# A decoder layer on one core: late blocks of attention keep the values as weights, search behind the low parts, every superblock splits its own weights

## The reference, cut to what matters

```
h = rms_norm(x);  proj = h @ w_in            # q, k, v, qi, ki, wi and the four HGRN parts
iscore[t,s] = sum_h wi[t,h] * relu(qi[t,h] . ki[s])          # 8 indexer heads of 64
idx = top_k(causal iscore, 256)                              # per query
o[t,h] = softmax(q[t,h] . k[idx] / 8) @ v[idx]               # 8 heads of 64, 2 KV heads
mix = concat(o, hgrn2(...)) @ w_out;   x = x + rms_norm(mix)
h2 = rms_norm(x);  ff = (silu(h2 @ w_gate) * (h2 @ w_up)) @ w_down       # inner width 2816
out = x + rms_norm(ff)
```

## Time and profile before

| | |
|---|---|
| median of 3 runs | 3363.38 us (3362.57 to 3368.68) |
| profiled execution | 3364.6 us |
| its span | 3362.8 us |
| mean granted TensorE clock | 0.984 |
| PE, PEld busy | 95%, 84% |
| DVE, ACT, POOL busy | 60%, 38%, 7% |
| HBM read and written | 393.41 MB, 132.71 MB |

### The profile page before, as it was taken

How to read it: one execution, slowest core, us unless ns; L and a number is a source line. 1 busy time by engine, 2 the same in 40 slices (tenths; PEclk the granted TensorE clock), 3 DMA queues, 4 the chain that set the end, 5 groups by cost and what they waited for, 6 DMA issues and landing times.

```text
span 3362.8 us, 46208 instructions
## 1 busy us (share of the span) xinstructions
PE 3198.6 (95%) x17928; PEld 2822.9 (84%) x17928; DVE 2020.8 (60%) x3427; ACT 1284.1 (38%) x2117; POOL 237.1 (7%) x400
## 2 busy tenths in 40 slices
PE   8999999999889899999889999998999999989998
PEld 7999999998777788878778888887888888868886
DVE  4467778788566776666676555567855653341223
ACT  3454445455466454444443333335433332210000
POOL 0001000000111110000110001011100000010000
PEclk9999999999899899999999999999999999989999
DMA  5543343443323556565643343345333333465554
GB/s 183 163 129 133 132 142 113 132 133 123 115 86 127 187 203 225 212 227 217 244 152 128 134 142 140 129 162 200 125 125 125 123 116 126 154 242 195 175 211 165
DMA packets 167658, 529.15 MB, mean 157 GB/s; under 512 B 17296, under 2 KB 38160, under 8 KB 165392
## 3 DMA queue, kind: packets, MB, share of 16 engines
q1 hardware_dynamic: 165136, 522.00, 44.9%
q10 hardware_dynamic: 2304, 4.20, 0.3%
HBM read 393.41 MB, written 132.71 MB: 156 GB/s over the span
## 4 chain that ended last, share of the span: by engine, by line
PE 58%; DVE 6%; DMA 5%; ACT 2%; issue 2%; SPq 0%; DVEq 0%; POOL 0%; ACTq 0%; POOLq 0%
PE PJ_d L2130 8%; PE PJ_d L2132 8%; PE PJ_d L2131 8%; PE SC L2083 6%; PE PJ_d L2155 6%; PE PJ_d L2157 6%; PE PJ_d L2156 6%; PE SA L2042 3%; PE SA L2069 3%; PE SA L2043 3%; DMA split_d<-wd 3%; DVE score L1773 1%; DVE prob L1867 1%; DVE h_lo L1887 1%; ACT h_hi L1645 1%
## 5 line engine op out<-in xcount | busy, mean ns | idle before, releaser
L2130 PE MATMUL PJ_d<-h_hi,wd 128*128 128x512 f32 (+1 forms) x1472 | 577.1, 392 | 12.7 <-DVE h_lo L1887 8.3
L2132 PE MATMUL PJ_d<-h_hi,wd 128*128 128x512 f32 (+1 forms) x1472 | 565.2, 384 | 0.0
L2131 PE MATMUL PJ_d<-h_lo,wd 128*128 128x512 f32 (+1 forms) x1472 | 564.2, 383 | 0.0
L733 PE MATMUL PJ<-w_hi,h_hi 128*128 128x338 f32 (+1 forms) x1280 | 416.9, 326 | 2.7 <-DVE w_lo L550 2.7
L734 PE MATMUL PJ<-w_lo,h_hi 128*128 128x338 f32 (+1 forms) x1280 | 409.4, 320 | 0.0
L735 PE MATMUL PJ<-w_hi,h_lo 128*128 128x338 f32 (+1 forms) x1280 | 409.3, 320 | 0.0
L1867 DVE CUSTOM_DVE_ANT_0 prob<-SA,bias 128x1024 f32<-128x1024 f32 (+7 forms) x192 | 170.0, 911 | 354.1 <-PE SA L2043 350.6
L1627 ACT ACTIVATE pT<-SA 128x512 f32<-128x512 f32 (+3 forms) x320 | 156.4, 531 | 571.5 <-PE SA L2069 571.5
L2130 PEld LDWEIGHTS PJ_d<-h_hi,wd 128*128 128x128 f32 x1472 | 281.5, 191 | 63.2 <-DVE wd L1882 5.2
L2132 PEld LDWEIGHTS PJ_d<-h_hi,wd 128*128 128x128 f32 x1472 | 280.8, 191 | 54.6
L2131 PEld LDWEIGHTS PJ_d<-h_lo,wd 128*128 128x128 f32 x1472 | 281.7, 191 | 49.0
(11 more groups left out here) (207 smaller groups left out, 5600.6 us busy)
## 6 DMA issues: line engine op xcount, KB each, us to landing
wd<-split_d SPq DMA_DIRECT2D x420, 512.0 KB, 3.8
split_d<-wd SPq DMA_DIRECT2D x140, 512.0 KB, 4.6
w_raw<-in_w_in SPq DMA_DIRECT2D x40, 684.0 KB, 4.5
w_raw<-in_w_in SPq DMA_DIRECT2D x40, 676.0 KB, 4.5
wd_land<-in_w_gu SPq DMA_DIRECT2D x88, 256.0 KB, 3.3
row_h<-proj_d SPq DMA_DIRECT2D x16, 1024.0 KB, 7.1
proj_d<-stage SPq DMA_DIRECT2D x40, 342.0 KB, 4.5
proj_d<-stage SPq DMA_DIRECT2D x40, 338.0 KB, 5.1
```

What stands on the lines that cost most here:

```text
L733: t.matmul(out, h_hi[:, k, tok], w_hi[:, u, e], start=(k == 0), stop=False)
L2130: t.matmul(to[:, tok], w_hi[:, r, w], h_hi[:, c, tok], start=(c == 0 and part != 1), stop=False)
L2131: t.matmul(to[:, tok], w_hi[:, r, w], h_lo[:, c, tok], start=False, stop=False)
L2132: last = t.matmul(to[:, tok], w_lo[:, r, w], h_hi[:, c, tok], start=False, stop=(c == KD - 1 and part != 0))
```

## The change

**Values.** In blocks 4 to 15 the values are the weights: a tile [128 keys x 128] holds, for one KV head, 64 columns of high and 64 of low parts; the moving operand is high and low of the turned probabilities side by side, 256 columns, in float32r. So `pT` gets a low half, made by DVE (`turned_probs_low`) from the transposes in PSUM behind ACT's copy. One product gives 128 x 256 in `SC`: rows are high and low dims, columns high and low tokens. ACT copies the columns of the low tokens (`copy_low_output`), DVE adds the others (`add_output`), and a product with a folded identity (`turn_output`) adds the low rows to the high and turns the result to tokens. DVE scales two heads at a time (`attention_pair`), SP stores them. Blocks 0 to 3 keep the old product (`values_early`).

**Where values live.** POOL splits each block's values (`split_values`), SP stores them to `v_d` and loads them twice a block in late blocks (`load_values`), once for each KV head, into four tiles; three of these lie in the space of the second row buffer. The row of a block therefore has one buffer from block 2 on and comes in two parts (`load_rest`, `load_q`), and POOL turns it in two parts (`prep_rest`, `prep_q`).

**Search.** On DVE the low parts of a head come before its search parts; in blocks with two pairs both search slots ("A" and "B") come behind the second low part, where "A" stood before the fill "B" until now.

**Weights.** `SPLIT_KEPT`, `split_d` and the stores are gone; all superblocks load raw units and split them on ACT and DVE.

```diff
-                for kb in range(4 * c, min(4 * c + 4, b + 1)):
-                    last = t.matmul(SC[:, h * HD:(h + 1) * HD], pT[:, m % 2, (kb % 4) * P:(kb % 4 + 1) * P],
-                                    V[:, kb, g * HD:(g + 1) * HD], start=(kb == 0), stop=(kb == b))
+                    pe.wait_ge(pt_low, m + 1 - TS * HEADS)
+                    if h % GROUP == 0:
+                        pe.wait_ge(*v_loaded[b, g, c])
...
+                    for kb in range(4 * c, min(4 * c + 4, b + 1)):
+                        last = t.matmul(SC[:, 0:2 * P], values_of(kb), pT[:, m % 2, kb % 4].rearrange("p n t -> p (n t)"),
+                                        start=(kb == 0), stop=(kb == b))
...
+            def turn_output(b, h):
...
+                t.matmul(SC[:, 2 * P + n % 2 * HD:2 * P + (n % 2 + 1) * HD], oT[:], folded, start=True, stop=True)\
+                 .then_inc(ot_turned, 1)
...
+            def copy_low_output(b, h):
...
+                s_.activation(oT[:], SC[:, P:2 * P], ACT.Copy).then_inc(ot_half, 1)
...
+            def turned_probs_low(b, h, p):
+                for c in range(2 * p, min(2 * p + 2, NCH(b))):
...
+                    dve.wait_ge(pt_ready, m + 1)
...
+                    v.tensor_tensor(to[:, :, 1, :], heads(of, w // P), to[:, :, 0, :].bitcast(F32), ALU.subtract).then_inc(pt_low, 1)
...
+            def add_output(b, h):
...
+                v.tensor_tensor(oT[:], SC[:, 0:P], oT[:], ALU.add).then_inc(ot_ready, 1)
...
                     fill(("A", b, h))
+                    for j in pairs_turned(b, h):
+                        attention_pair(b, j)
+                    if not early(b):
+                        turned_probs_low(b, h, 0)
+                    if pairs_of(b) == 2:
+                        fill(("B", b, h))
+                        turned_probs_low(b, h, 1)
                     for k in search(b, h, "A"):
                         topk_part(b + 1, k)
-                    fill(("B", b, h))
+                    if pairs_of(b) == 1:
+                        fill(("B", b, h))
                     for k in search(b, h, "B"):
                         topk_part(b + 1, k)
                     fill(("C", b, h))
...
-                if u not in split_no:
...
-                    sp.dma_start(w_two[:, u % RING].bitcast(F32), split_d[at]).then_inc(w_in[u % RING], 16)
-                    return
...
-            def store_split(u):
-                sp.dma_start(split_d[at], w_two[:, u % RING].bitcast(F32)).then_inc(split_stored[u % RING], 16)
...
+            def load_values(b, g):
...
+                for c in range(NCH(b)):
+                    if v_before[b, g, c]:
+                        sp.wait_ge(pv_done, v_before[b, g, c])
...
+                    sp.dma_start(v_tiles[c][:, 0:last - 4 * c, :].bitcast(F32), v_d[g, :, 4 * c:last, :])
```

More of the change, by code:

```diff
@@ L955, in mixer_phase @@
                 unit_last[unit_no[u]] = n
[L956 to L969, removed]
     loads_after, split_step = {}, dict(enumerate((0, 0, 1, 1, 3, 4, 5, 6)))
@@ L1462, in after @@
                     load_unit(u)
-                for u in stores_after.get(n, []):
-                    store_split(u)
             def fill(key):
@@ L1492, in _ @@
                         fill((name, b, h))
-            store(NB - 1)
+                    for j in pairs_turned(b, h):
+                        store(b, j)
+            after(TAIL[0])
+            store(NB - 1, HEADS // 2 - 1)
             load_mix(NS - 1, 3)
-            for n in range(*TAIL):
+            for n in range(TAIL[0] + 1, TAIL[1]):
                 after(n)
@@ L1500, in _ @@
                 store_out(NS - 1, i)
[L1501 to L1503 removed]
+            sp.wait_ge(stored, stored_upto(NB - 1))
             for i in range(TS):
@@ L1716, in _ @@
                             fill(("O", b, 0))
+                    if not early(b) and h >= 1:
+                        copy_low_output(b, h - 1)
                     fill(("A", b, h))
@@ L2002, in _ @@
                         scores(b, h + 1)
+                    if not early(b) and h >= 1:
+                        add_output(b, h - 1)
                     for key in openings(b, h):
@@ L2036, in open_split @@
                 for h, c0 in enumerate(first):
-                    last = t.transpose(pair(key)[0:rows_of(key), h * P:(h + 1) * P], row[:, b % 2, c0:c0 + rows_of(key)],
+                    last = t.transpose(pair(key)[0:rows_of(key), h * P:(h + 1) * P], row_of(b)[:, c0:c0 + rows_of(key)],
                                        ident[:])
@@ L2071, in turn_probs, with values_early @@
                 last.then_inc(sa_full, 1)
+            def values_early(b, h):
+                g, m = h // GROUP, pt_order[b, h, 0]
+                pe.wait_ge(pt_ready, m + 1)
+                if m == 0:
+                    pe.wait_ge(value0_ready, 1)
+                if b >= 1 and h == 0:
+                    pe.wait_ge(att_early, b)
+                for kb in range(b + 1):
+                    last = t.matmul(SC[:, h * HD:(h + 1) * HD], pT_early[:, m % 2, kb * P:(kb + 1) * P],
+                                    V_early[:, kb, g * HD:(g + 1) * HD], start=(kb == 0), stop=(kb == b))
+                last.then_inc(pv_done, 1)
@@ L2195, in _ @@
                         turn_probs(b, h, p)
+                        if p == 0 and h >= 1:
+                            turn_output(b, h - 1)
                         fill(("BC"[p], b, h))
                         values(b, h, p)
-            for n in range(*TAIL):
+            item(TAIL[0])
+            turn_output(NB - 1, HEADS - 1)
+            for n in range(TAIL[0] + 1, TAIL[1]):
                 item(n)
```

330 lines of the change are left out of this document (222 added, 108 removed).

## The result

The changed kernel takes **3448.5 us** (median of 4, 3445.6 to 3450.7) against 3363.0 us for the kernel before on the same chip: a ratio of 1.026 [1.023, 1.028]. The forecast was 3375 us and its range ended at 3445 us, so the change is slower, as the likeliest sign had it, but by 85 us and not by 10. The time lies 3.5 us from the 3445 that rival B gave. The profiled execution has a span of 3443.8 us, 81.0 more than before.

What follows compares the result with a forecast made beforehand. PE, busy 95%, was taken to set the time nearly everywhere, DVE in blocks 4, 8 and 12. -4 - 17 + 35 - 10 + 5 + 1 = +10 us on 3364.6, median 1.2 lower: 3375 us, range 3305 to 3445.

Steps and rivals of the forecast that it cites:

- the likeliest sign: Whole kernel: slower than the 3356.7 to 3370.1 us that counts as no change, chance 0.54.
- rival B: Blocks 8 to 14: DVE, busy 0.80 at most, sets the time; +97 us there, 3445 us in all; chance 0.24.
- The values on PE: Blocks 4 to 15: 256-column products 0.119 us apart instead of 0.216; PE needs 77 us less after added output turns.
- Rival C: Value products on PE: 256 columns cost what the float32 product did; 77 us come back, 3452 us; chance 0.03.
- the usual blocks: Blocks 9, 10, 11, 13, 14: PE gains 39 us, late values take 22 back, -17 us in all.
- 5 x 4.5 = 22: Five usual blocks: PE's values late behind DVE's search parts, 4.5 us a block, bounds 0 and 10.
- blocks 4 to 7: -13 us from PE, +9 of new waits, half of it in block 4: -4 us.
- 15 and tail: Block 15, without search, gains 10 us; the tail loses 5 to splits in its opening chain of norms.
- blocks 8 and 12: Superblock borders: DVE's 150 and 174 us plus 20 us idle give 170 and 194, so +14 and +21 us.
- The splits of 420 more units: Raw weights split on DVE and ACT: 85 us of DVE in blocks 8 to 11, 12 to 15 and tail each.
- The DMA part: Smaller loads, no split stores: 0 in usual blocks, up to 9 us back in block 8; values loads cost 0.
- PE waiting for low parts, most behind heads 0, 4 and 6: Expected in the profile after: a new wait of PE for DVE's low parts, several us a block.

Runs made afterwards that it cites:

- e9: Changed kernel; value products take the high half twice; DVE's low part does the same work on a constant, waiting for nothing: 3374.2 us, ratio 1.004.
- e11: Changed kernel; value products take the high half twice; DVE's low part keeps its wait but works on 4 columns of each 128: 3405.7 us, ratio 1.013.
- e10: Changed kernel; value products take the high half twice, still 256 columns; DVE's low parts removed, neither wait nor work: 3326.5 us, ratio 0.990.
- e2: Kernel before, with raw weights in all superblocks and no stores of split units: 3358.5 us, ratio 0.999.
- e1: Changed kernel with the old weights path back (superblock 0 splits and stores, 1 to 3 load split units): 3438.8 us, ratio 1.023.

## Why the prediction was wrong

**The values on PE: right.** The products of 256 columns start 0.120 us apart (median), forecast 0.119, and the turns of an output take 0.14 us a head where 0.22 was costed, so PE gained nearer 85 us than 77. Rival C fell. The Trainium skill (FP8 and Floating Point Precision, TensorE Precision Notes) states that true FP32 takes 4 passes; by passes and columns alone the new product would cost as much as the old, and the trace has 0.120 against 0.216 us.

**The wrong step is the usual blocks.** The term "5 x 4.5 = 22" was to hold all that the new order costs there, and DVE's standing in front of its low parts was put at nothing in it. Lengths from DVE's first scores of a block to those of the next, as differences to before:

| stretch | forecast | changed | e9: work alone | e11 | e10 |
|---|---|---|---|---|---|
| blocks 4 to 7 | -4 | +1 | +4 | -3 | -9 |
| 9, 10, 11, 13, 14 | -17 | **+34** | -16 | +16 | -30 |
| block 8 | +14 | +23 | +14 | +17 | +1 |
| block 12 | +21 | +34 | +20 | +21 | +10 |
| 15 and tail | -5 | -11 | -12 | -9 | -11 |

(By PE's first scores, which come before DVE's, the changed kernel has +27 in the usual blocks and -5 in the last row.) In the blocks from 8 to 14 the forecast is within 1 us of the kernel with DVE's work and without its wait (e9: 3374.2 us against 3375). Some of that is luck: blocks 4 to 7 and the tail are 8 and 7 us off and cancel, and the 22 us that were counted for late values are in e9 14 us of DVE's work (against e10) and 9 us of the 39 that e10 lacks already. The prediction added a head's new work to DVE (16.3 and 12.7 us against 15.8 of PE) and asked only how late PE's values would come, 4.5 us a block. It never asked how long DVE would stand in front of a low part. In block 13 that is 18.1 us, 2.3 a head:

```profile
DVE pT L1982 <- ACT pT L1716: 18.1, 11, 2.6
```

With that on top of the prediction's sums (35/8 x 0.61 in them is 2.7, not 2.5, which changes little), DVE needs 18.6 us in a head with two search parts and 15.0 in one with a single part, so the heads with two parts overrun PE's 15.8 by 2.8 us and the others have nearly nothing left to catch up with. 20 us idle were granted to blocks 8 and 12, for just this chain, and none to the usual ones. PE's gain there was 7.8 us a block (39 over five) and the blocks grew by 6.9 (34 over five), so the loss is 14.7 us a block in place of the 4.5 of the forecast, above the 8 from which rival B was said to decide; in e9, where DVE does not stand, it is 4.6. B's number came true, but not wholly its mechanism: 0.80 is not the most that DVE can hold. e9 has DVE at 0.85 in block 13 at 179 us; the changed kernel stops at 0.79, with 18.1 us of its 191 spent standing in front of low parts.

**Blocks 8 and 12** came out 9 and 13 us longer than forecast, and e9 has the forecast's 14 and 20, so the excess goes with the same wait. With PE's pauses comes a term that the sum lacked altogether: **the clock**. By each kernel's clock record, behind 1100 us PE runs at the lower level (1.2 GHz) for 82 us in the kernel before, 163 in the changed one, 138 in e11, 122 in e9 and 81 in e10. Blocks 8 and 12 have 31 us of it before, 89 in the changed kernel and 68 in e9. PE's pauses (starts more than 0.45 us apart, less the 0.23 of a product) grew from 92 to 214 us over the same stretch. 122 us of pauses and half of 81 us at the lower level make 163; less the 77 to 85 that PE gained that is 78 to 86, against 81 measured in the span. It is a rough sum: for some 24 of the 81 us PE stands anyway, and they are counted in both terms, so the clock is worth 29 to 41 us.

**The rest.** The splits of 420 more units: 85 us in blocks 8 to 11 and as many in 12 to 15 were counted as if they were as dear as the low parts. They wait for little that is late, and from block 8 on they cost 5 us in the kernel before (e2) and 35 in the changed one (e1). The DMA part put the end of the stores at 0 but for up to 9 us in block 8; the runs give 20 us in blocks 4 to 7 of the changed kernel and 8 in those of the kernel before, and there the forecast of -4 came out as +1. Block 15 gained 8 us (forecast 10). The tail is 3 us shorter where 5 longer was forecast. "PE waiting for low parts, most behind heads 0, 4 and 6" came as 27.2 us, third among PE's waits.

**What stays open.** e11 keeps two things together: DVE standing in its order, and the PSUM pair held until DVE has read it. No kernel here separates them; none of PE's waits in the changed kernel names a low part as the reader of a held pair (0.4 us in e11), which speaks for the order, but this is a reading and not an experiment. Nor was a low part tried that DVE takes up one head later.

## What to carry to other kernels

When work is added to an engine whose stream is in fixed order, cost the time it stands in front of the new instruction beside the time it runs: here 288 operations of 0.62 us cost 48 us as work and about 66 as waits. An engine that had 350 us of waits took 255 us of splits that wait for little at 5 us, and lost 114 with 167 us that hang on another engine's last result; beside those the same splits cost 35. And read an experiment by stretches: e1's small gain was a loss of 20 us in one place and a gain of 35 in another. Ask first whether a second pass for precision is needed at all: without it the same change is 2% faster than the kernel before (how much precision that gives up is not shown here).

## What the runs showed of the hardware

A stall costs more than its length. Around one in block 12 of the changed kernel (PE timeline, then windows of the stall, of what follows, and later):

```profile
2501.10 0.69 PE L2257 MATMUL SC<-xt,oT 128*128 128x64 f32 x2 [7.72 <-DVE oT L1995]
...
2502.55 0.63 PE L2188 MATMUL SA<-KT,qiT 128*128 128x512 f32 x1
2502.97 0.63 PE L2189 MATMUL SA<-KT,qiT 128*128 128x512 f32 x1
...
2506.16 0.39 PE L2301 MATMUL PJ_d<-h_lo,wd_hi 128*128 128x512 f32 x1
2506.39 0.40 PE L2302 MATMUL PJ_d<-h_hi,wd_lo 128*128 128x512 f32 x1
```

```profile
2493.00:2501.00 8.00, 0.38 (x2) 0.00 (x0) 7.16 (x11) 0.00 (x0) 6.62 (x21) 0.66 0.43 144
2501.00:2508.60 7.60, 7.50 (x24) 6.08 (x25) 6.79 (x11) 1.71 (x3) 0.30 (x2) 0.68 0.05 15
2508.60:2520.00 11.40, 11.40 (x51) 9.26 (x50) 7.96 (x8) 6.83 (x9) 0.00 (x0) 1.00 0.22 67
```

PE stands 7.7 us; the granted clock is 0.66 and then 0.68 of full in the two windows, and products of 512 columns start 0.42 us apart until 2505.9 and 0.23 after it. The 11 or so products in between cost 2.2 us on top of the pause, and PE's busy time hides it: it counts 7.50 of 7.60 us there.

The number of columns hardly sets the price of a short product: 128 columns start 0.111 us apart and 256 columns 0.120, so the second half of the probabilities was nearly free on TensorE (9 us for 1008 products). Nearly all of its price lay with the engine that had to make it and add it.
